# Building the relative-position bias table on chip in eight parts, and loading gate rows from SyncE

## The reference, cut to what matters

```
sh, sc, gt = jnp.split(jax.nn.silu(c) @ w_ada[l] + b_ada[l], 3, axis=-1)
h = rms_norm(x, norm_g[l]) * (1 + sc[:, None]) + sh[:, None]
...
dr = key_rows - r[:, None] + (WIN_H - 1)
dc = jnp.clip(cidx[None, :] - cidx[:, None] + (WIN_W - 1), 0, 2 * WIN_W - 2)
bias = rpb[:, dr[:, None, :, None], dc[None, :, None, :]]
...
s_nb = s_nb + bias.astype(jnp.float32)[None]
s_nb = jnp.where(in_win[:, None, :], s_nb, -jnp.inf)
...
x = x + gt[:, None] * y
```

## Time and profile before

| | us |
|---|---|
| median of three runs | 1320.16 (1316.65 to 1321.74) |
| the profiled execution | 1321.37 |
| its span, first to last instruction | 1319.6 |
| PE busy | 1173.3 (89%) |
| DVE busy | 661.2 (50%) |
| ACT busy | 602.2 (46%) |
| POOL busy | 246.6 (19%) |
| mean granted TensorE clock | 0.946 |
| DMA, mean over the span | 120 GB/s |

### The profile page before, as it was taken

One profiled execution on the slowest core, in us unless ns is written; L12 is line 12 of the kernel. 1 busy time (PEld: TensorE's weight loads), 2 busy tenths in 40 slices (PEclk: granted clock), 3 DMA queues, 4 the chain that ended last, 5 costly groups with the idle time before them and its releaser, 6 DMA issues.

```text
span 1319.6 us, 16761 instructions
## 1 busy us (share of the span) xinstructions
PE 1173.3 (89%) x5973; PEld 913.3 (69%) x5973; DVE 661.2 (50%) x1225; ACT 602.2 (46%) x1174; POOL 246.6 (19%) x322
## 2 busy tenths in 40 slices
PE   4785789989987997889998899998979999999987
PEld 0463467767665776668777677887768887888885
DVE  0543254453465264464445566655466556465543
ACT  0442145444475144456456463444454445544553
POOL 4155032128001213030230103000012111121100
PEclk9897789999998889899989999998979999999999
DMA  8647234332402222322220385553436665444401
GB/s 227 226 122 147 85 114 119 126 112 80 160 1 84 69 76 70 90 65 80 64 74 7 117 286 150 187 172 127 162 128 191 185 182 164 127 120 121 140 1 49
DMA packets 79474, 158.62 MB, mean 120 GB/s; under 512 B 5910, under 2 KB 6206, under 8 KB 79136
## 3 DMA queue, kind: packets, MB, share of 16 engines
q1 hardware_dynamic: 74992, 145.82, 35.5%
q0 software_dynamic: 4400, 11.73, 4.3%
HBM read 154.39 MB, written 3.78 MB: 120 GB/s over the span
## 4 chain that ended last, share of the span: by engine, by line
PE 73%; DVE 7%; ACT 7%; DMA 4%; POOL 4%; issue 3%; SPq 1%; ACTq 0%; POOLq 0%; DVEq 0%
PE bank L654 17%; PE bank L656 16%; PE bank L655 16%; PE bank L794 5%; PE bank L769 3%; PE bank L779 3%; PE bank L871 2%; DVE w_lo L1533 2%; POOL small L1393 2%; PE bank L844 2%; DMA raw<-in_w_ada_dram 2%; ACT w_hi L969 2%; PE bank L856 1%; DMA work<-in_w_ada_dram 1%; PE bank L604 1%
## 5 line engine op out<-in xcount | busy, mean ns | idle before, releaser
L654 PE MATMUL bank<-w_lo,h_hi 128*128 128x512 f32 (+1 forms) x1152 | 466.1, 405 | 29.8 <-DVE h_lo L1596 15.6
L656 PE MATMUL bank<-w_hi,h_hi 128*128 128x512 f32 (+1 forms) x1152 | 451.0, 392 | 0.0
L655 PE MATMUL bank<-w_hi,h_lo 128*128 128x512 f32 (+1 forms) x1152 | 450.5, 391 | 0.0
L1533 DVE TENSOR_TENSOR w_lo<-raw,w_hi 128x1024 fp32r<-128x1024 f32 x224 | 285.1, 1279 | 312.5 <-ACT w_hi L969 310.8
L969 ACT ACTIVATE w_hi<-raw 128x1024 fp32r<-128x1024 f32 x224 | 235.9, 1058 | 331.1 <-PE bank L656 281.1
L654 PEld LDWEIGHTS bank<-w_lo,h_hi 128*128 128x128 f32 x1152 | 224.7, 195 | 91.5 <-issue 42.5
L656 PEld LDWEIGHTS bank<-w_hi,h_hi 128*128 128x128 f32 x1152 | 223.7, 194 | 45.9
L655 PEld LDWEIGHTS bank<-w_hi,h_lo 128*128 128x128 f32 x1152 | 225.4, 196 | 41.1 <-issue 0.2
L794 PE MATMUL bank<-work,stage 128*128 128x128 f32 x640 | 92.0, 285 | 1.8 <-ACT stage L1156 1.6
L1156 ACT ACTIVATE stage<-bank 128x512 f32<-128x512 f32 (+1 forms) x96 | 50.3, 524 | 77.2 <-PE bank L779 77.0
L794 PEld LDWEIGHTS bank<-work,stage 128*128 128x128 f32 x640 | 82.7, 199 | 3.4 <-ACT stage L1156 2.8
(11 more groups left out here) (169 smaller groups left out, 1095.5 us busy)
## 6 DMA issues: line engine op xcount, KB each, us to landing
raw<-in_b_w_in_dram SPq DMA_DIRECT2D x80, 512.0 KB, 3.7
raw<-in_w_in_dram SPq DMA_DIRECT2D x56, 512.0 KB, 4.0
raw<-in_a_w_in_dram SPq DMA_DIRECT2D x48, 512.0 KB, 4.2
raw<-in_w_ada_dram SPq DMA_DIRECT2D x32, 512.0 KB, 3.9
work<-in_w_ada_dram SPq DMA_DIRECT2D x16, 512.0 KB, 14.2
raw<-in_w_out_dram SPq DMA_DIRECT2D x16, 512.0 KB, 3.5
raw<-in_a_w_out_dram SPq DMA_DIRECT2D x16, 512.0 KB, 3.5
raw<-in_b_w_out_dram SPq DMA_DIRECT2D x8, 512.0 KB, 3.5
```

What stands on the lines that cost most here:

```text
L654: pe.matmul(bank, hT(h_hi, ph, kt, tt), w_lo[:, s, k, lo:lo + w], start=first, stop=False)
L655: pe.matmul(bank, hT(h_lo, ph, kt, tt), w_hi[:, s, k, lo:lo + w], start=False, stop=False)
L656: mm = pe.matmul(bank, hT(h_hi, ph, kt, tt), w_hi[:, s, k, lo:lo + w], start=False, stop=last)
L1533: dve.tensor_tensor(w_lo[:, i % SPLIT, :, :], raw[:, PIECE_AT[p] % RAW, :, :], w_hi[:, i % SPLIT, :, :].bitcast(F32), ALU.subtract).then_i ...
```

## The change

The prefill of `bias` and the shifted writes into it are gone. SP loads the 84 lines of `nat_rpb` that are used into 84 partitions of `work`, in 12 small transfers, after entry 8 of the list and after a wait for the end of chunk 0 (the place in `work` was a weight buffer until then). POOL sets two buffers of 8 by 96 to zero, then copies the 31 numbers of a line eight times, each one place further right, and stores these eight query columns for all 84 lines (252 KB). It does so eight times at eight places of its order between chunks 1 and 3, in the two buffers by turns, and for most of them waits for the end of a tile's projection, and for the store of two parts before. The places outside the 31 hold zero instead of -1e30; the window mask covers them as before. `load_bias` waits for the last two parts. The three gate rows are issued by SP, after entries 9, 10 and 12. The modulation products themselves (`ada_row`, `ada_half` and their totals) are the same in both kernels, and the diff does not touch them.

```diff
--- before.py
+++ after.py
@@ -27,7 +27,10 @@
 BIAS_W = GRID_W + 2 * WIN_W
 ROWS = 56 + 2 * 24
 STAGE_W = 6144
+WORK_W = 20736
 RPB_LINES = 7
+BIAS_LINES = 2 * C_HEADS * RPB_LINES
+SKEW_ROWS = 8
 GMLP = 2 * D
 GROUPS = 8
 DIL = 3
@@ -49,6 +52,9 @@

 FOLLOWING = {"out0": "in1", "out1": "gin", "gout": "din", "dout": None}

+BIAS_ROWS_AT = [(1, 1), (1, 2), (1, 3), (2, 0), (2, 1), (2, 2), (3, 0), (3, 1)]
+BIAS_ROWS_AFTER = {1: ("in0", 0, 3), 2: ("in0", 0, 3), 3: ("in0", 1, 0), 4: ("in0", 1, 2), 5: ("in0", 2, 0), 6: ("in0", 2, 2), 7: ("in0", 2, 3)}
+
 TURNED_AFTER = {(2, 0): 0, (2, 1): 1, (3, 0): 2, (3, 1): 3}

 
@@ -75,6 +81,9 @@

 ADA_READY = {p: was[:2] for p, was in zip(pieces_of("in0")[5:], ADA_BESIDE.values()) if was[2] == 3}
 ADA_HALF = {p: (*was[:2], was[2] // 2) for p, was in ADA_BESIDE.items() if was[2] % 2}
+
+
+GATE_ROW_AFTER = {9: 0, 10: 1, 12: 2}

 
 def first_pieces():
@@ -229,7 +238,7 @@
         x = sb("x", [P, 4, D])
         h_hi = sb("h_hi", [P, 4096], F32R)
         h_lo = sb("h_lo", [P, 4096], F32R)
-        work = sb("work", [P, 20736])
+        work = sb("work", [P, WORK_W])
         stage = sb("stage", [P, STAGE_W])
         ident = sb("ident", [P, P])
         gains = sb("gains", [P, 2, 384])
@@ -253,6 +262,8 @@
         vals = region(7168, (4, V_W))
         gate = region(10240, (4, D))
         nat_bias = region(14336, (C_HEADS, 6, GRID_W))
+        skewed = [work[0:BIAS_LINES, 14336 + SKEW_ROWS * BIAS_W * i:14336 + SKEW_ROWS * BIAS_W * (i + 1)] for i in range(2)]
+        rpb_lines = work[0:BIAS_LINES, 14336 + 2 * SKEW_ROWS * BIAS_W:14336 + 2 * SKEW_ROWS * BIAS_W + RPB_W]
         ada_gate = region(16640, (3, D))
         ada_sum = region(19712, (NC,))
         cpad = region(20224, (KT, 32))
@@ -293,7 +304,6 @@
         out_part = [st(5120, 512), st(5632, 512)]

         rows = stage[0:ROWS, 4608:4608 + P]
-        far = stage[0:2 * C_HEADS * RPB_LINES, 4736:4736 + BIAS_W]
         lam = st(4832, 256).rearrange("p (f l d) -> p f l d", f=4, l=2)

 
@@ -316,10 +326,10 @@

         landed = [sem(f"landed{i}", 16) for i in range(RAW)]
         start_loads = {n: sem(f"loaded_{n}", 16) for n in (
-            "rows", "x", "ctx", "tab", "mask", "gains", "lambdas", "gate_bias", "bias", "ln", "ws",
+            "rows", "x", "ctx", "tab", "mask", "gains", "lambdas", "rpb", "gate_bias", "bias", "ln", "ws",
             "post", "dil_tab", "dil_mask")}
         stored = sem("stored", 16)
-        bias_out = sem("bias_out", 16)
+        bias_out = [sem(f"bias_out{i}", 16) for i in range(2)]
         setup_v, setup_p, setup_a, setup_t = sem("setup_v"), sem("setup_p"), sem("setup_a"), sem("setup_t")
         weights_hi, weights_lo, piece_used = sem("weights_hi"), sem("weights_lo"), sem("piece_used")
         ada_landed = {p: sem(f"ada_landed{i}", 16) for i, p in enumerate(ada_pieces(0, range(4)))}
@@ -564,6 +574,17 @@
                 sp.dma_start(raw[:, n % RAW, :, :], weight_source(p)).then_inc(*landed[n % RAW].at(p))
                 if n == 2:
                     sp.dma_start(x[:, 2:4, :], a["ctx"][0].rearrange("(t p) d -> p t d", p=P)).then_inc(*start_loads["ctx"].at(0))
+                if n == 8:
+                    sp.wait_ge(*projected.seen(("in0", 0, 3)))
+                    for layer in range(2):
+                        for h in range(C_HEADS):
+                            at = (layer * C_HEADS + h) * RPB_LINES
+                            sp.dma_start(rpb_lines[at:at + RPB_LINES, :], a["nat_rpb"][layer, h, WIN_H - 4:WIN_H + 3, :]) \
+                                .then_inc(*start_loads["rpb"].at((layer, h)))
+                if n in GATE_ROW_AFTER:
+                    row = GATE_ROW_AFTER[n]
+                    sp.dma_start(ada_gate[:, row, :], a["b_ada"][row // 2:row // 2 + 1, 2 * D:3 * D].broadcast_to([P, D])) \
+                        .then_inc(*start_loads["gate_bias"].at(row))
             o = out[0].rearrange("(t p) d -> t p d", p=P)
             for tt in X_TILES:
                 sp.wait_ge(*added.seen(("dout", 1, tt)))
@@ -1345,31 +1366,27 @@
                     pool.dma_start(lam[:, i, layer, :], a[name][layer:layer + 1, :].broadcast_to([P, 32])) \
                         .then_inc(*start_loads["lambdas"].at((i, layer)))

-            def bias_in_dram():
-
-
-                pool.memset(far[:, :], NEG).then_inc(*setup_p.at("far"))
-                pool.wait_ge(*setup_p.seen("far"))
-                lines = 2 * C_HEADS * RPB_LINES
-                pool.wait_ge(*projected.seen(("in0", 0, 3)))
-                pool.dma_start(a["bias"], far[:, :].unsqueeze(1).broadcast_to([lines, GRID_W, BIAS_W])).then_inc(*bias_out.at("far"))
-                for row in range(3):
-                    pool.dma_start(ada_gate[:, row, :], a["b_ada"][row // 2:row // 2 + 1, 2 * D:3 * D].broadcast_to([P, D])) \
-                        .then_inc(*start_loads["gate_bias"].at(row))
-
-            def bias_lines():
-
-                pool.wait_ge(*bias_out.seen("far"))
-                for layer in range(2):
-                    for h in range(C_HEADS):
-
-                        dst = bass.AP(a["bias"].tensor, (layer * C_HEADS + h) * RPB_LINES * GRID_W * BIAS_W + 1,
-                                      [[GRID_W * BIAS_W, RPB_LINES], [BIAS_W + 1, GRID_W], [1, RPB_W]])
-                        src = a["nat_rpb"][layer, h, WIN_H - 4:WIN_H + 3, :].unsqueeze(1).broadcast_to([RPB_LINES, GRID_W, RPB_W])
-                        pool.dma_start(dst, src).then_inc(*bias_out.at((layer, h)))
+            def bias_rows(k):
+
+                if k == 0:
+                    pool.wait_ge(*start_loads["rpb"].seen((1, C_HEADS - 1)))
+                    for i in range(2):
+                        pool.memset(skewed[i], 0.0).then_inc(*setup_p.at(("skew_zero", i)))
+                    pool.wait_ge(*setup_p.seen(("skew_zero", 1)))
+                else:
+                    pool.wait_ge(*projected.seen(BIAS_ROWS_AFTER[k]))
+                if k >= 2:
+                    pool.wait_ge(*bias_out[k % 2].seen(k - 2))
+                to = bass.AP(work, 14336 + SKEW_ROWS * BIAS_W * (k % 2) + SKEW_ROWS * k + 1,
+                             [[WORK_W, BIAS_LINES], [BIAS_W + 1, SKEW_ROWS], [1, RPB_W]])
+                pool.tensor_copy(to, rpb_lines.unsqueeze(1).broadcast_to([BIAS_LINES, SKEW_ROWS, RPB_W])).then_inc(*setup_p.at(("skewed", k)))
+                pool.wait_ge(*setup_p.seen(("skewed", k)))
+                pool.dma_start(a["bias"][:, SKEW_ROWS * k:SKEW_ROWS * (k + 1), :], skewed[k % 2].rearrange("p (q w) -> p q w", w=BIAS_W)) \
+                    .then_inc(*bias_out[k % 2].at(k))

             def load_bias(layer):
-                pool.wait_ge(*bias_out.seen((1, C_HEADS - 1)))
+                for i in range(2):
+                    pool.wait_ge(*bias_out[i].seen(GRID_W // SKEW_ROWS - 2 + i))
                 for b in range(2):
                     for h in range(C_HEADS):

@@ -1445,8 +1462,8 @@
                         process_in(ph, c - 1, (n + 2,))
                         if n == 3:
                             process_in(ph, c, (0, 1))
-                        if (ph, c, n) == ("in0", 1, 3):
-                            bias_lines()
+                        if ph == "in0" and (c, n) in BIAS_ROWS_AT:
+                            bias_rows(BIAS_ROWS_AT.index((c, n)))
                         if (ph, c, n) == ("in0", 3, 3):
                             load_bias(0)

@@ -1466,7 +1483,6 @@

             norm("in0")
             make_tabs(0)
-            bias_in_dram()
             project_in("in0")
             mask_bias(0)
             diff_norm(0)
```

## The result

The changed kernel takes 1301.95 us in the median of four runs (1301.44 to 1304.65), the kernel before 1318.76 us in four runs beside it (1316.65 to 1321.74). The ratio is 0.9875, with a 95% interval of 0.9849 to 0.9901: 16.8 us less. The forecast was 16.9 us less.

A forecast was written before the change was run, and what follows sets the result against it. Late weight loads behind POOL's DMA traffic were taken to bound PE; 3.9 + 9.9 + 3.1 = 16.9 us off 1321.37 gives 1304.5, or 1303.3 us against the median. The range was 1296 to 1310.5 us.

The forecast's parts named there:

- What bounds it: Two PE waits of gate products for late weight loads, 22.8 us together, in chunk 1, lengthened by POOL's DMA traffic.
- The first hole: PE idle 12.38 us before 109.25 us; entry 11 issued 1.6 earlier, landing 2.3 shorter: 3.9 us gained, 8.4 left.
- The second hole and the clock: PE idle 10.39 us before 136.61 us: 9.9 gained without shifted writes, plus 3.1 from the half-clock stretch behind it.
- One step: At the second gate products only a late load can hold PE; entry 15's cover is 0.4 us, so 0.5 us stays.
- what is late next: After both holes: PE itself, then its 2.82 us wait for the first scores, which moves earlier unchanged.
- Added work: SP's twelve small loads, at most 5.5 us, and gate rows; POOL's parts, 1.5 us each: hidden, nothing booked.
- (a): Rival: parts and a gate row delay entry 15; a 5.5 us second hole, gain 8.8 us, 1311.4 us; chance 0.15.
- (b): Rival: twelve small loads hold SP for 27 us, entry 11 lands late; gain 4 us, 1316 us; chance 0.03.
- (c): Rival: parts stored at the shifted writes' pace, 7.7 us each, delay eight weight loads; slower, 1334 us; chance 0.04.
- (d): Rival: power no earlier or landing stays 6.17 us at entry 11, the rest comes; within range, no separate chance.
- The others: Remaining signs: gate-product waits 8.4 and below 1 us, power 0.1 us behind sum, entry 11 at 101.3, chunk 2 clock 1.00.

The follow-up runs named there:

- the parts in a row: The kernel after, with all eight table parts at one place at the end of chunk 1, without waits for tiles: 1302.27 us, ratio 0.9868.
- one experiment: The kernel after, with two DVE splits moved ahead of a scale that waits for POOL, in chunk 1 only: 1304.12 us, ratio 0.9881.

## Why the prediction was right, step by step

**What bounds it** held in both halves. The two waits for loads were 22.8 us before and are 8.3 after. The fill and the gate rows lengthened the first, the shifted writes made the second. The runs that change one thing at a time show it: leaving out the writes gives 11.7 us and leaves the first hole, moving the gate rows gives 3.5 (2.6 us at the first hole in its profile), and the table alone (fill and writes) gives 16.2, as good as all. One reading ahead of the prediction was wrong and changed nothing in it: the first eighth of the span holds 55.4 of PE's 146.3 us of idle time, over a third of it and not most.

**The first hole.** Forecast 3.9 us: 1.6 on the issue, 2.3 on the landing. From the mark to the first gate products it was 109.25 - 85.70 = 23.6 us and is 105.65 - 86.19 = 19.5, 4.1 us less, and the hole is 8.29 us for 8.4 forecast. The power starts 0.08 us behind the sum and the landing takes 3.8 us: 1.6 us on the issue and 2.5 on the landing, both terms within 0.2 us of the forecast.

**The second hole and the clock.** Forecast 9.9 and 3.1 us. From the first to the second gate products it was 27.36 us and is 16.93, 10.4 less, and from there to the scores 20.70 and 17.86, 2.8 less. Of the 10.4, 9.4 are the hole (10.39 to 1.03) and 1.1 are clock, which I had booked at nothing. Behind the first hole it is back up at 109.6 us (0.80 in the window from 108 to 112), 4 us after the restart, where it took some 6 before. So the hole gave 0.5 us less than forecast and the clock 0.8 more (1.1 and 2.8 for 3.1), and these two misses partly cancel in the sum.

**One step was wrong in kind.** I wrote that nothing but a late load can hold the gate products, and I left 0.5 us of the second hole because the cover of entry 15 is thin. The load was never late. What stands there is ACT, which loads a table and copies five more tiles before it frees the bank that PE needs, 1.03 us; before, this lay under the hole. ACT in after:

```profile
119.25 1.28 ACT L1074 ACT_TABLE_LOAD   x1
120.55 1.49 ACT L1074 ACTIVATE work<-bank 128x256 f32<-128x256 f32 x5
121.88 0.65 ACT L1107 ACTIVATE work<-bank 128x512 f32<-128x512 f32 x1
```

I had named PE itself as what is late next, and that was wrong by this 1 us. It could have been read in the trace of before, in ACT's order of time: its last copy of a turned tile ends at 127.21, 1.0 us behind the turn's end on PE, inside the hole.

```profile
126.56 0.65 ACT L1086 ACTIVATE work<-bank 128x512 f32<-128x512 f32 x1
```

**Added work** cost nothing, as booked. Twelve small loads took 4.18 us of SP for 5.5 at most. A copy took 0.39 to 0.59 us, inside my bounds of 0.35 and 1.5 and below the 0.7 I used; the part ahead of a power was hidden, since POOL still waited 0.70 us at 180.20. A part landed in 3.6 us.

**The rivals.** (a), contention moves to the parts, fails in after, and fails even with the parts in a row. (b), SP held by small loads, fails at 0.35 us each. (c) fails by the 3.6 us in which a part lands, and (d), a first hole as before, by the 8.29 us. The Trainium skill, DMA: Bandwidth & Descriptors, section Rules for kernel authors, says to make many small transfers one. Here twelve small ones cost nothing while they were covered, and with 36 the cost came from what they pushed together, not from themselves. By the earlier trace rows 54 KB took 10.2 us in the median as the shifted writes, against 252 KB in 3.6 us as lines of 3 KB. That is no test of the rule: the writes differ from the parts in number and size, in the length of their runs, in their shifted places, and in their source, which is DRAM and not `work`.

**What the sum leaves open.** The three steps make 17.4 us in the profiles, from the mark to the first scores, and 17.1 in the second profile of after. It is the better measure of the forecast. The medians give 16.8 us in one set of runs and 14.9 in another (1319.81 - 1304.94), so the 16.9 of the forecast was met more closely than this kernel can be measured. The two profiled executions differ by 19.8. The other 2.4 us (2.9, as the mark of after comes 0.5 us later) lie behind the changed stretch, where PE's order is the same. Windows of before, after and the second profile of after, each from the first load of `w_out` of layer 0 to the last load of `w_in` of layer 1, show it: length, busy times, granted clock.

```profile
351.70:636.30 284.60, 248.31 (x1372) 196.44 (x1373) 146.98 (x335) 139.12 (x334) 49.94 (x60) 0.93 0.24 71
```

```profile
335.20:616.60 281.40, 244.86 (x1372) 194.19 (x1373) 146.98 (x335) 139.12 (x334) 50.09 (x60) 0.95 0.24 72
```

```profile
336.40:620.70 284.30, 247.65 (x1372) 196.02 (x1373) 146.90 (x335) 139.53 (x334) 50.05 (x60) 0.93 0.24 71
```

The stretch takes 3.2 us less in the one profile of after, at a clock of 0.95, and is back at 284.3 us and 0.93 in another profile of the same kernel. So these 3 us are the clock's chance and no part of the gain, as the range allowed for. Two signs of the prediction were missed by it: a mean granted clock of 0.95 or more (it is 0.949, 0.946 before), and no change behind 160 us but the offset. The others came out, entry 11's issue included (101.83 for 101.3, with a mark 0.5 us later).

## What to carry to other kernels

Ask of a late load both when it was issued and how long it took to land: here part of one hole was issue and nearly all of the other landing, and different traffic made each. Look at the pieces of a transfer and not only at its bytes: twelve writes of 54 KB in short shifted runs held up 512 KB loads that share the engines, at both places tried, and assembling the same data on chip into long lines cured it at once. Which property of the writes makes them dear, no run here separates. And before a wait is removed, look for the second-latest condition of the same instruction: it took the place of most of the gain in one experiment, and no list of waits had shown it while the first wait covered it.

## What the runs showed of the hardware

In the shifted writes the DMA engines are busy to the full while they move very little: 45 GB/s at a share of 1.08. A weight load of 512 KB that meets them takes 14.6 to 18 us instead of 3.9. The list of DMA queues of before, for 84 to 110 us (the fill and the gate rows) and for 110 to 134 us (the shifted writes), gives packets, MB and the share of the 16 engines that POOL's queue took:

```profile
q0 software_dynamic: 1008, 3.64, 46.0%
```

```profile
q0 software_dynamic: 563, 0.69, 52.1%
```

The packets of the writes took 12.5 us of all engines for 0.69 MB, those of the fill and the gate rows 12.0 us for 3.64 MB. So it is not the bytes. By the code the fill has as many rows, 84 x 64 = 5376 of 384 bytes, as the writes have runs, 12 x 448 of 124 bytes, and it took less than those 12.0 us, since the gate rows are in them. The number of pieces may be the larger part of the cost, then, but not all of it: their length, their shifted places and their source in DRAM remain, and no run here tells these apart.

An idle stretch of 2.82 us before the scores goes with a fall of the clock in before, in after and in all eleven other profiles, while how long PE then works at the lower level differs: about 6 us behind the first hole of before, 4 behind that of after. The same kernel, after, took 1301.4 to 1304.7 us in one set of runs and 1304.8 to 1305.3 in another, with medians 3.0 us apart; differences of 3 us between kernels are to be read only within a set.
